# Five filter taps, one rounding remainder and one norm sum placed elsewhere in a two-layer trunk kernel

## What is computed

```python
def conv_recurrent_mixer(hn, w_in, conv_a_w, conv_a_b, ...):
    u = hn @ w_in
    a_val, a_gate, xr, gr = jnp.split(u, [D_A, 2 * D_A, 2 * D_A + D_B], axis=-1)
    ya = a_val * jax.nn.sigmoid(a_gate)
    ya = causal_depthwise_conv(ya, conv_a_w, conv_a_b)      # 31 taps
    ya = jax.nn.silu(layer_norm(ya, ln_a_g, ln_a_b))
    xr = causal_depthwise_conv(xr, conv_b_w, conv_b_b)      # 4 taps
    yb = rg_lru(xr, ...) * jax.nn.gelu(gr)
    return jnp.concatenate([ya, yb], axis=-1) @ w_out
```

## Time and profile before

| | |
|---|---|
| median of 3 runs | 2348.19 us (2347.66 to 2349.77) |
| profiled execution, its own time | 2347.8 us |
| span of its trace | 2346.1 us |
| TensorE busy with matmuls | 2324.9 us (99%) |
| VectorE busy | 1534.6 us (65%) |
| ScalarE busy | 1252.6 us (53%) |
| GpSimd busy | 77.1 us (3%) |
| mean granted TensorE clock | 0.998 of full speed |

### The profile page before, as it was taken

One profiled execution on the slowest core, in us unless ns is written; L12 is line 12 of the kernel. 1 busy time (PEld: TensorE's weight loads), 2 busy tenths in 40 slices (PEclk: granted clock), 3 DMA queues, 4 the chain that ended last, 5 costly groups with the idle time before them and its releaser, 6 DMA issues.

```text
span 2346.1 us, 39851 instructions
## 1 busy us (share of the span) xinstructions
PE 2324.9 (99%) x13964; PEld 2078.5 (89%) x13964; DVE 1534.6 (65%) x1848; ACT 1252.6 (53%) x1616; POOL 77.1 (3%) x73
## 2 busy tenths in 40 slices
PE   8999999999999999999999999999999999999998
PEld 7999998888888888888888888888888888888887
DVE  8899776556556555668676666765555555556666
ACT  6876655445445435556666666555444444445454
POOL 0046100000000000000000000000000000000000
PEclk9999999999999999999999999999999999999999
DMA  8555465655655665665555555565556556556553
GB/s 254 181 181 161 154 206 172 195 179 190 194 189 182 191 199 179 188 205 174 186 179 157 176 170 177 180 190 179 189 196 188 180 194 198 179 184 202 186 166 122
DMA packets 432334, 431.24 MB, mean 184 GB/s; under 512 B 13312, under 2 KB 430208, under 8 KB 432256
## 3 DMA queue, kind: packets, MB, share of 16 engines
q1 hardware_dynamic: 431968, 429.97, 58.1%
q10 hardware_dynamic: 288, 0.23, 0.0%
HBM read 428.05 MB, written 2.10 MB: 183 GB/s over the span
## 4 chain that ended last, share of the span: by engine, by line
PE 97%; DVE 1%; ACT 1%; DMA 1%; issue 0%; DVEq 0%; ACTq 0%; SPq 0%
PE ps L492 54%; PE ps L498 28%; PE ps L533 3%; PE ps L534 3%; PE ps L535 3%; PE ps L490 2%; PE ps L497 1%; PE O L803 1%; DVE spl L1337 1%; DMA raw<-in_w_o 0%; PE O L654 0%; PE Z L628 0%; ACT spl L861 0%; PE Z L637 0%; PE ps L707 0%
## 5 line engine op out<-in xcount | busy, mean ns | idle before, releaser
L1337 DVE TENSOR_TENSOR spl<-raw,spl 128x1024 fp32r<-128x1024 f32 x797 | 938.6, 1222 | 579.5 <-ACT spl L861 572.2
L861 ACT ACTIVATE spl<-raw 128x1024 fp32r<-128x1024 f32 (+1 forms) x811 | 817.3, 1054 | 686.5 <-PE ps L498 593.7
L492 PE MATMUL ps<-XA,spl 128*128 128x512 f32 x2816 | 705.0, 392 | 7.3 <-DVE spl L1545 6.7
L492 PE MATMUL ps<-XB,spl 128*128 128x512 f32 x2784 | 711.5, 392 | 0.0
L492 PEld LDWEIGHTS ps<-XA,spl 128*128 128x128 f32 x2816 | 505.1, 189 | 91.5 <-issue 7.4
L492 PEld LDWEIGHTS ps<-XB,spl 128*128 128x128 f32 x2784 | 491.4, 188 | 75.6
L498 PEld LDWEIGHTS ps<-XB,spl 128*128 128x128 f32 x2784 | 394.5, 191 | 39.0
L498 PEld LDWEIGHTS ps<-XA,spl 128*128 128x128 f32 x2816 | 387.3, 191 | 31.4
L498 PE MATMUL ps<-XB,spl 128*128 128x256 f32 x2784 | 402.6, 281 | 0.0
L498 PE MATMUL ps<-XA,spl 128*128 128x256 f32 x2816 | 393.8, 282 | 0.0
L1373 DVE TENSOR_TENSOR tv<-cross,ps 128x512 f32<-128x512 f32 x181 | 123.2, 681 | 13.2 <-ACT cross L861 13.0
(11 more groups left out here) (207 smaller groups left out, 1531.6 us busy)
## 6 DMA issues: line engine op xcount, KB each, us to landing
raw<-in_w_up SPq DMA_DIRECT2D x256, 512.0 KB, 4.8
raw<-in_w_down SPq DMA_DIRECT2D x256, 512.0 KB, 5.2
raw<-in_w_qkv SPq DMA_DIRECT2D x96, 512.0 KB, 4.4
raw<-in_w_gate SPq DMA_DIRECT2D x64, 512.0 KB, 4.6
raw<-in_w_in SPq DMA_DIRECT2D x63, 512.0 KB, 4.7
raw<-in_w_out SPq DMA_DIRECT2D x32, 512.0 KB, 3.6
raw<-in_w_o SPq DMA_DIRECT2D x32, 512.0 KB, 4.8
raw<-in_w_proj SPq DMA_DIRECT2D x8, 512.0 KB, 4.1
```

The source lines that it names most:

```text
L492: pe.matmul(ps[:, b + o, :], w[:, q, 0, c], x[:, kt, :, :], start=start, stop=False)
L861: return act.activation(out, in_, ACT.Copy, scale=scale)
L1337: dve.tensor_tensor(s[:, :, 1, :], raw[:, m % NRAW, :, :], s[:, :, 0, :].bitcast(F32), ALU.subtract).then_inc(lo_ready, 1)
```

## The change

`TAPS_PE` goes from 14, 14, 14, 12 to 13, 12, 12, 12: one tap of pair 0, two of pair 1 and two of pair 2 go from TensorE (L803, with their diagonal matrices at L1174) to VectorE's second sum. The remainder of `yb` leaves VectorE; GpSimd does it as two subtractions of 128 x 1024, one behind its third turn (n = 2, the end of pair 0's sums) and one behind its sixth (n = 5, the end of pair 1's). Each raises `yb_tiles` by one, so the first chunk of an output group waits for one half, the second for both. The second `ln_mean` goes from ahead of output group 6 to between its two chunks.

```diff
-TAPS_PE = (14, 14, 14, 12)
+TAPS_PE = (13, 12, 12, 12)
@@ gpsimd, at the end of a turn n
+                if n in (2, 5):
+                    t = 4 * (n // 3)
+                    pool.wait_ge(rg_act, 11)
+                    pool.tensor_tensor(XB[:, t + 8:t + 12, 1, :], pp[:, t:t + 4, :],
+                                       XB[:, t + 8:t + 12, 0, :].bitcast(F32), ALU.subtract).then_inc(yb_tiles, 1)
@@ tensor
-            mids = {0: lambda: conv(2, 2, 3), 4: lambda: ln_mean(1)}
+            mids = {0: lambda: conv(2, 2, 3), 4: lambda: ln_mean(1), 6: lambda: ln_mean(2)}
             for s in range(NG):
-                if s == 6:
-                    ln_mean(2)
-                small_gemm(G_OUTB + s, C_OUTB + 2 * s, XB, [(yb_tiles, 1), (yb_tiles, 1)], (8, 12), mids.get(s))
+                small_gemm(G_OUTB + s, C_OUTB + 2 * s, XB, [(yb_tiles, 1), (yb_tiles, 2)], (8, 12), mids.get(s))
@@ vector, glu_pair
-                    if c == 1 and q == 6:
-                        dve.wait_ge(rg_act, 11)
-                        lo_of(XB, 8, 8, pp[:, 0:8, :]).then_inc(yb_tiles, 1)
```

## The result

The changed kernel takes 2354.27 us (median of ten runs, 2352.49 to 2356.61) against 2348.80 us before (ten runs, 2347.66 to 2351.10): 5.5 us longer, ratio 1.0023 with a 95% interval of 1.0013 to 1.0033. The forecast was 2346.2 us, in a range that ended at 2348.8. The profiled execution took 2352.64 us with a span of 2350.6, at the low end of the runs.

The account below looks back on a forecast made before the run. TensorE, 97% of the chain, was taken as the bound, with one 1.69 us hole. Taps gave -1.97 us, all other terms 0: 2347.8 - 1.97 = 2345.8, plus 0.39 to the median, 2346.2 us; range 2344.4 to 2348.8.

Parts of the forecast that it names:

- Taps off TensorE: TensorE's list ahead of output group 1: five taps less at 0.394 us each, 1.97 us saved.
- Taps onto VectorE: VectorE's second sum: five more taps add 1.25 us, the lower value of 1.25 to 1.95.
- The remainder on GpSimd: Two halves in GpSimd's idle times, collisions with VectorE taken as 0; bounds 0 and 5.8 us.
- the dearer case: Two halves each stretch a VectorE split by 0.73 us; 1.46 less 0.95 covered widens the hole by 0.51 us.
- Whether the hole moves: TensorE's 1.69 us idle time before the first norm sum, waiting for `nacc`, moves along with TensorE and stays; effect 0.
- The second norm sum: Put one chunk later, within output group 6: gains nothing, cost 0 to 0.15 us, taken as 0.
- GpSimd locks VectorE out: Rival: VectorE's two-input instructions wait a whole half each, 5.8 us, between 163 and 191 us; 2351.1 us; chance 0.05.
- slower by over 0.2%: Whole kernel measurably slower than before, by a lock worse than reckoned; chance 0.04.

Follow-up runs that it names:

- halves after gates and sum later: Changed kernel with GpSimd's two halves held until the GLU gates of pairs 1 and 2 are done, first norm sum ahead of output group 5: 2346.33 us.
- the remainder back on VectorE: Changed kernel with the remainder of yb as one subtraction on VectorE again, five taps and second norm sum as changed: 2352.37 us.
- halves after gates: Changed kernel with only GpSimd's two halves held back until the GLU gates of pairs 1 and 2 are done on VectorE: 2350.22 us.
- halves in gaps: Changed kernel with GpSimd's halves held back, first behind pair 1's GLU gate, second behind the split of step 6 of the second pair: 2352.02 us.
- halves only: Kernel before with only the remainder of yb moved, as two halves on GpSimd; taps and second norm sum as before: 2351.64 us.

## Why the prediction was wrong

**Taps off TensorE: right, a little too small.** Not 0.394 but 0.43 us a tap: what follows a series starts before the series has ended (154.59 against 152.62 + 2.33 = 154.95), so a series must be compared with a shorter one (five taps 1.97, four 1.54, three 1.11), not divided. Five taps are 2.15 us, and they came through to within 0.2 us in the version with halves after gates and sum later.

**Taps onto VectorE: right.** From the third gate to the fourth VectorE took 25.92 us before and 28.51 after; less the stretch of 2.07 us more at one split, two taps cost 0.52, as the 1.25 us for five had it. What they move was left out: with the remainder back on VectorE these 1.25 us alone made a split second to a remainder of weights, and cost 3.42.

**The remainder on GpSimd: the step that failed.** It was taken at 0, "since taps are most of what VectorE does there", with 0.51 us as the dearer case. Measured are 7.77 us on VectorE. Three things were wrong in it. The 0.73 us of the earlier trace rows was read as the price of a collision with the sums from 157.16, when it is only what was left of the GpSimd subtraction ahead of them as VectorE came to it at 156.33 (GpSimd's timeline of the kernel before):

```profile
154.79 2.40 POOL L463 TENSOR_TENSOR spl<-raw,spl 128x1024 fp32r<-128x1024 f32 x1
```

It ends at 157.19, and the split at 158.28, 1.09 us behind. The price is the rest of the other engine's instruction, up to 2.2 us here; the trace before had shown it once nearly whole, on GpSimd's side, in the 3.40 us at 205.78. Two collisions were counted, at the two halves, and there were six. GpSimd's first remainder of weights in pair 1 came 2.67 us earlier than before (166.15 against 168.82), VectorE's split, held up by the half at the gate, only 0.99 (167.25 against 168.24), and was second where it had been first; and the one that VectorE had been ahead of by 0.2 us before caught it as well. And the product of a gate and the sum into `nacc`, which stand among the taps, have two inputs in SBUF as well. By gates VectorE gained 2.82 us in pair 0, lost 5.96 in pair 1 and 2.59 in pair 2: 5.73 us late at the fourth gate, where the sum had it 1.49 early at the output groups behind.

**Whether the hole moves: the place was wrong.** The prediction followed `nacc` back and found that TensorE itself times it from 226 us on, which holds in the changed kernel, where the hole is 1.68 us. But there TensorE had been held back ahead of it; where the wait ahead of the taps was 2.30, 2.23, 0.89 or 0.23 us, the hole was 2.71, 2.71, 3.23 or 2.72. The prediction did not ask for the first place at which TensorE needs VectorE on time. That is the fourth gate, before pair 3's taps (VectorE's timeline of the kernel before, then TensorE's):

```profile
216.95 0.69 DVE L1736 TENSOR_TENSOR glu<-glu,tv 128x512 f32<-128x512 f32 x1 [0.77 <-ACT tv L1128]
```

```profile
220.82 1.46 PE L803 MATMUL O<-glu,dg 128*128 128x256 f32 x6
```

From 217.64 to 220.82 are 3.18 us of slack, 1.03 once TensorE is 2.15 us earlier. 5.73 - 1.03 = 4.70 us is the wait, measured 4.77.

**The second norm sum: right,** shown by its own run.

**A term that was missing.** The lower clock level behind a wait, 1.69 us here.

**The rivals.** "GpSimd locks VectorE out" was the mechanism, with 0.05. Its price was 5.8 us on VectorE (7.77), its place the first norm sum (the fourth gate), its time 2351.1 us (2354.27, the clock being left out). That the two sums on VectorE lie so near is luck: at the two halves, the only places it had, 3.05 us were lost, and four collisions that it did not count made up the rest. The rule cited with it, of the Trainium skill, SBUF — State Buffer, section "Who interferes with whom", describes what the trace shows to within 0.15 us: with two inputs in SBUF VectorE waits until GpSimd's instruction has ended. It had been set aside on one row that was misread. The chance of slower by over 0.2%, 0.04, was too small: 0.23% was measured, though the interval reaches down to 0.13%. The range had no room for it.

**Still open.** The bill accounts for 4.3 us of two profiled executions, and the medians lie 5.5 apart. The runs of one kernel spread by 2 to 7 us, and the profile shows one of them; that collisions decided by 0.1 us fall this way or that would fit, but was not shown. Why the part before the first tap varies by 3.4 us was not tried.

## What to carry to other kernels

Work that is moved to GpSimd is costed by when it starts against VectorE's two-input instructions: take for each the whole rest of GpSimd's instruction, and let it start behind an event of VectorE that is followed by work with one SBUF input. An engine that is 97% of the chain still hangs on the engine that feeds it, so follow each of the feeder's results, not only the one that waits today, and write down the slack of each. Where instructions of the two engines come close in time, look at who came first and by how much: 0.2 us of luck is a term of the sum.

## What the runs showed of the hardware

Idle time of TensorE can cost more than itself. Behind idle times of 4.61, 8.17 and 3.23 us the granted clock fell to the lower level, and 1.5 to 1.7 us were lost; behind 4.73 us it was 2.17. Behind 1.7 us, in three kernels, it stayed at 1.00. Between the two it was not settled by length in these runs: 2.19 us cost 1.46 (granted clock 0.50 over the next 3 us), and 2.71 and 2.72 us ahead of the norm sum cost 1.50 with the remainder back on VectorE and with halves after gates, while the same 2.71 us with halves in gaps, and 2.30 and 2.23 us ahead of the taps, cost nothing, with the clock at 1.00. The Trainium skill, TensorE: Matmul & The Clock Gate, section "What's actually happening", says that the full clock is granted for activity and withdrawn in idleness; the rows agree that far. A hole that is cheap now may cost nearly four times its growth when it grows by half a microsecond, as in the run with halves only: 0.5 us of hole, 1.96 of time in the stage.

VectorE and GpSimd keep each other out both ways. A split that starts behind a GpSimd subtraction ends 1.07 to 1.09 us behind its end, and a GpSimd subtraction that starts 0.2 us behind a split takes 3.37 to 3.40 us instead of 2.40. Taps, with one input in PSUM, keep their 0.47 to 0.48 us beside the same subtractions.
